# One sum of a vector over the partitions by two rounded matmuls instead of an exact one, in a two-layer hybrid decoder on one Trainium2 core

## The reference

```python
c_act = jax.nn.silu(c)
for i in range(DEPTH):                       # 2 layers
    mod = c_act @ ada_w[i] + ada_b[i]        # 1024 -> 9 * 1024
    sh1, sc1, gt1, sh2, sc2, gt2, sh3, sc3, gt3 = jnp.split(mod, N_MOD, axis=-1)
    h = h + 0.5 * gt1 * swiglu(modulate(h, sh1, sc1), ffn_w_gu[i, 0], ffn_w_down[i, 0])
    h = h + gt2 * mixer(modulate(h, sh2, sc2))
    h = h + 0.5 * gt3 * swiglu(modulate(h, sh3, sc3), ffn_w_gu[i, 1], ffn_w_down[i, 1])
# swiglu: gate, up = split(x @ w_gu); (silu(gate) * up) @ w_down, with D_FF = 2816
```

## Time and profile before

| | us |
|---|---|
| median of three runs (1491.93, 1502.3, 1502.09) | 1502.09 |
| the profiled execution | 1490.03 |
| its span | 1488.3 |
| PE busy | 1277.8 (86%) |
| DVE busy | 959.1 (64%) |
| ACT busy | 542.0 (36%) |

### The profile page before, as it was taken

The page is one execution under the profiler, slowest core; times in us unless marked ns, Lnnn a source line. Parts: engine busy times, 40 slices in busy tenths (PEclk is TensorE's granted clock), DMA queues, the critical chain, the costliest instruction groups (busy, mean ns, idle before and its releaser), DMA issues.

```text
span 1488.3 us, 17063 instructions
## 1 busy us (share of the span) xinstructions
PE 1277.8 (86%) x6370; PEld 1017.5 (68%) x6370; DVE 959.1 (64%) x1242; ACT 542.0 (36%) x733; POOL 77.9 (5%) x68
## 2 busy tenths in 40 slices
PE   5899998785988999989999868775836995899998
PEld 1588887662566888867888744664835994688886
DVE  5787776876448877768787563367592338554553
ACT  2434345342344344354343434352501002344431
POOL 1000000000000000000000000005350005000000
PEclk9899999895589999999999987887756555999999
DMA  8798874830018988757888541310102011465551
GB/s 310 250 316 299 295 253 149 282 114 1 0 57 283 313 299 291 263 189 267 291 303 296 143 121 57 113 57 1 29 0 57 2 58 58 140 226 170 169 198 57
DMA packets 186753, 252.17 MB, mean 169 GB/s; under 512 B 31489, under 2 KB 122625, under 8 KB 186689
## 3 DMA queue, kind: packets, MB, share of 16 engines
q1 hardware_dynamic: 186690, 251.32, 50.3%
HBM read 249.19 MB, written 2.10 MB: 169 GB/s over the span
## 4 chain that ended last, share of the span: by engine, by line
PE 72%; DVE 17%; DMA 4%; ACT 4%; issue 2%; SPq 2%; POOL 0%; DVEq 0%; ACTq 0%; POOLq 0%
PE bank L709 18%; PE bank L711 18%; PE bank L710 18%; DVE inv_tmp L1795 2%; DVE gu_lo L1610 2%; DVE ada_acc L1543 2%; PE bank L910 2%; PE bank L1120 2%; PE bank L682 1%; PE bank L1128 1%; PE bank L768 1%; ACT gu_hi L1178 1%; PE bank L920 1%; PE bank L937 1%; DVE inv_out L1797 1%
## 5 line engine op out<-in xcount | busy, mean ns | idle before, releaser
L709 PE MATMUL bank<-gu_hi,xT_hi 128*128 128x512 f32 (+1 forms) x880 | 352.4, 400 | 32.1 <-DVE gu_lo L1610 10.8
L710 PE MATMUL bank<-gu_lo,xT_hi 128*128 128x512 f32 (+1 forms) x880 | 350.1, 398 | 0.0
L711 PE MATMUL bank<-gu_hi,xT_lo 128*128 128x512 f32 (+1 forms) x880 | 349.5, 397 | 0.0
L1610 DVE TENSOR_TENSOR gu_lo<-raw,gu_hi 128x2048 fp32r<-128x2048 f32 (+1 forms) x116 | 257.6, 2255 | 60.7 <-ACT gu_hi L1178 60.7
L1178 ACT CAST gu_hi<-raw 128x2048 fp32r<-128x2048 f32 (+1 forms) x116 | 215.4, 1884 | 36.1 <-DMA raw<-in_ffn_w_gu_dram 23.5
L709 PEld LDWEIGHTS bank<-gu_hi,xT_hi 128*128 128x128 f32 x880 | 170.8, 194 | 74.5 <-issue 14.6
L710 PEld LDWEIGHTS bank<-gu_lo,xT_hi 128*128 128x128 f32 x880 | 170.7, 194 | 37.4 <-issue 0.7
L711 PEld LDWEIGHTS bank<-gu_hi,xT_lo 128*128 128x128 f32 x880 | 170.5, 194 | 35.9
L1543 DVE SCALAR_TENSOR_TENSOR ada_acc<-ada_raw,cact,ada_acc 128x512 f32<-128x512 f32 x224 | 168.4, 752 | 12.3 <-DMA ada_raw<-in_ada_w_dram 1.0
L709 PE MATMUL bank<-dn_hi,hT_hi 128*128 128x512 f32 x320 | 142.9, 447 | 2.6 <-DVE dn_lo L1620 2.6
L1196 ACT ACTIVATE hid<-bank 128x256 f32<-128x256 f32 x88 | 33.3, 380 | 291.3 <-PE bank L711 291.3
(11 more groups left out here) (267 smaller groups left out, 1619.2 us busy)
## 6 DMA issues: line engine op xcount, KB each, us to landing
raw<-in_ffn_w_gu_dram SPq DMA_DIRECT2D x176, 512.0 KB, 9.0
ada_raw<-in_ada_w_dram SPq DMA_DIRECT2D x128, 512.0 KB, 6.9
raw<-in_ffn_w_down_dram SPq DMA_DIRECT2D x40, 1024.0 KB, 5.0
raw<-in_rwkv_w_rkv_dram SPq DMA_DIRECT2D x24, 512.0 KB, 5.2
raw<-in_dsa_w_in_dram SPq DMA_DIRECT2D x16, 512.0 KB, 5.0
front<-in_ada_w_dram SPq DMA_DIRECT2D x8, 512.0 KB, 8.0
front<-in_ada_w_dram SPq DMA_DIRECT2D x4, 1024.0 KB, 13.8
last_raw<-in_ffn_w_down_dram SPq DMA_DIRECT2D x4, 1024.0 KB, 6.4
```

Source lines behind the costliest of these rows:

```text
L709: nc.tensor.matmul(out_ap, sta_hi, mov_hi, start=start, stop=False, skip_group_check=True)
L710: nc.tensor.matmul(out_ap, sta_hi, mov_lo, start=False, stop=False, skip_group_check=True)
L711: return nc.tensor.matmul(out_ap, sta_lo, mov_hi, start=False, stop=stop, skip_group_check=True)
L1610: nc.vector.tensor_tensor(gu_lo[:, par, ks, 0:width], buf[:, i, 0:4 * width].rearrange("p (k c) -> p k c", k=4), gu_hi[:, par, ks, 0:width ...
```

## The change

Three things change.

1. In the FFNs (not in the attention) the sum over the partitions is made by two matmuls in the rounded format. ACT casts `ada_acc` to `acc_hi` (`round_acc`), DVE subtracts to get `acc_lo` (`rest_of_acc`), and PE multiplies a rounded matrix of ones by both (`ffn_total`). `acc_hi` and `acc_lo` lie in the place of `xn`. `round_acc` stands on ACT ahead of `round_down`, `rest_of_acc` on DVE ahead of `rest_of_down`.
2. Before the first FFN, vector 3 has four products on PE and four on DVE instead of two and six; vector 2 is loaded in one transfer instead of two; the second half of weight block 0 is split (ACT and DVE) ahead of `first_x(2)` and `first_x(3)` instead of behind them; on PE the sum of vector 3 and two transposes move by a few matmuls.
3. At the entry of the third FFN, `ffn(2)`, ACT casts the second weight block around `deviation(q, 1)` instead of behind `turned_tile(q, 1)`.

```diff
-    FRONT_PIECES = (4, 2, 2, 4)
-    ON_PE = 2
+    FRONT_PIECES = (4, 2, 1, 4)
+    ON_PE = (2, 2, 2, 4)
+            def ffn_total(f, b):
+                u = ADA_DONE[f] + b
+                pe.wait_ge(acc_ready, u + 1)
+                nc.tensor.matmul(TB[0][:], ones_r[:], acc_hi[:], start=True, stop=False)
+                nc.tensor.matmul(TB[0][:], ones_r[:], acc_lo[:], start=False, stop=True).then_inc(ada_sum, 1)
@@ first_gate_up (PE)
-                gate_up(0, 0, 0, ks=range(0, 2))
+                gate_up(0, 0, 0, ks=range(0, 4))
                 front_total(3)
-                gate_up(0, 0, 0, ks=range(2, 4))
                 pe.wait_ge(xT_ready, 2)
-                gate_up(0, 0, 1, ks=range(0, 2))
-                turn_x(0, range(2, 3))
-                gate_up(0, 0, 1, ks=range(2, 4))
-                turn_x(0, range(3, 4))
+                gate_up(0, 0, 1, ks=range(0, 4))
+                turn_x(0, range(2, 4))
@@ ffn, step (PE)
                             pe.wait_ge(hT_ready[0], ub)
-                            ada_total(v0 + b - 1, TB[0])
+                            ffn_total(f, b - 1)
                         down(f, ub - 1, 0, peeled and b == 1)
@@ ACT
+            def round_acc(v):
+                act.wait_ge(ada_step, (v - ADA_FRONT) * KD + KD)
+                nc.scalar.copy(acc_hi[:], ada_acc[:]).then_inc(acc_hi_ready, 1)
@@ ffn (ACT)
+                if f == 2:
+                    act.wait_ge(g_ready[1], n0)
+                    round_block(n0 + 1, (n0 + 1) % 2, free=True, halves=range(0, 1))
                 if f:
                     deviation(q, 1)
+                if f == 2:
+                    round_block(n0 + 1, (n0 + 1) % 2, free=True, halves=range(1, 2))
+                if f:
                     turned_tile(q, 1)
@@ step (ACT)
                         silu(n - 1, ub - 1, 1, peeled and ub == 1)
                         round_hidden(ub - 1, 0, peeled and ub == 1)
+                        if nv and not (peeled and b > nv):
+                            round_acc(v0 + b - 1)
                         round_down(f, ub - 1, peeled and ub == 1)
-                    round_block(n + 1, (n0 + odd + 1) % 2, peeled and n == 0)
+                    if not (peeled and b == 0 and f == 2):
+                        round_block(n + 1, (n0 + odd + 1) % 2, peeled and n == 0)
@@ start (ACT)
             round_block(0, 0, True, halves=range(0, 1))
+            round_block(0, 0, True, halves=range(1, 2))
             copy_mods(3, FRONT[3][0], TB[1])
-            round_block(0, 0, True, halves=range(1, 2))
@@ first_modulate (DVE)
                 front_products(3)
+                rest_of_block(0, 0, halves=range(1, 2))
                 dve.wait_ge(mods_ready, 4)
                 first_x(2)
                 first_x(3)
-                rest_of_block(0, 0, halves=range(1, 2))
@@ step (DVE)
+            def rest_of_acc(f, b):
+                dve.wait_ge(acc_hi_ready, ADA_DONE[f] + b + 1)
+                nc.vector.tensor_tensor(acc_lo[:], ada_acc[:], acc_hi[:].bitcast(F32), ALU.subtract).then_inc(acc_ready, 1)
                         rest_of_hidden(ub - 1, 0)
+                        if nv and not (peeled and b > nv):
+                            rest_of_acc(f, b - 1)
                         rest_of_down(f, ub - 1)
```

More of the change, by code:

```diff
@@ L64, in trunk @@
     FRONT = ((2, 0), (0, 2), (3, 1), (1, 3))
-    FRONT_PIECES = (4, 2, 2, 4)
-    ON_PE = 2
+    FRONT_PIECES = (4, 2, 1, 4)
+    ON_PE = (2, 2, 2, 4)
     ADA_FFN = ((4, 10), (17, 10), (27, 9), (36, 0))
+    ADA_DONE = tuple(sum(n for _, n in ADA_FFN[:f]) for f in range(4))
     ADA_DSA = 14
@@ L116, in trunk @@
         chunk_decay = place("chunk_decay", [P, KD, NC])
+        ones_r = place("ones_r", [P, P], F32R, at=top["at"])
         rstat = place("rstat", [P, 128])
@@ L127, in trunk @@
         xn_at = top["at"]
+        acc_hi = place("acc_hi", [P, HALF], F32R, at=xn_at)
+        acc_lo = place("acc_lo", [P, HALF], F32R, at=xn_at + 2048)
         xn = place("xn", [P, 2, HALF])
@@ L140, in trunk @@
         front_acc = [ada_acc[:], hid[:].rearrange("p t c -> p (t c)")]
-        c_wide = place("c_wide", [P, 2, P], at=spare_at)
+        c_wide = place("c_wide", [P, ON_PE[-1], P], at=spare_at)
         last_raw = place("last_raw", [P, 2, D], at=ada_at)
@@ L231, in trunk @@
         ada_sum = sem("ada_sum")
+        acc_hi_ready = sem("acc_hi_ready")
+        acc_ready = sem("acc_ready")
         mods_ready = sem("mods_ready")
@@ L688, in front_products @@
                     pe.wait_ge(mods_ready, j - 1)
-                pe.wait_ge(front_in[j][0], 16)
-                for k in range(ON_PE):
+                for k in range(ON_PE[j]):
+                    if k % 2 == 0:
+                        pe.wait_ge(front_in[j][k * len(front_in[j]) // KD], 16)
                     nc.tensor.matmul(spread[:], c_wide[:, k, :], front[:, FRONT[j][1], k, :], start=k == 0, stop=False)
             def front_total(j):
-                pe.wait_ge(front_step, (j + 1) * (KD - ON_PE))
+                pe.wait_ge(front_step, sum(KD - n for n in ON_PE[:j + 1]))
                 nc.tensor.matmul(TB[j % 2][:], ones[:], front_acc[j % 2], start=False, stop=True).then_inc(ada_sum, 1)
+            def ffn_total(f, b):
[3 more added lines that the diff above has]
+                nc.tensor.matmul(TB[0][:], ones_r[:], acc_lo[:], start=False, stop=True).then_inc(ada_sum, 1)
             def turn_x(q, parts=range(4)):
@@ L837, in ffn @@
                     pe.wait_ge(hT_ready[0], last)
-                    ada_total(v0 + nv - 1, TB[0])
+                    ffn_total(f, nv - 1)
                 down(f, last - 1, 0, False)
@@ L1153, in _ @@
             pe.wait_ge(consts, 6)
-            pe.wait_ge(c_ready, 2)
+            pe.wait_ge(c_ready, 3)
             for j in range(3):
@@ L1475, in ffn @@
                 round_hidden(last - 1, 0)
+                if nv == NB - 1:
+                    round_acc(v0 + nv - 1)
                 round_down(f, last - 1, False)
@@ L1498, in _ @@
             nc.scalar.activation(cact[:], ccol[:], ACT.Silu).then_inc(c_ready, 1)
-            nc.scalar.activation(c_wide[:], ccol[:, 0:ON_PE].unsqueeze(2).broadcast_to([P, ON_PE, P]), ACT.Silu
+            nc.scalar.activation(c_wide[:], ccol[:, 0:ON_PE[-1]].unsqueeze(2).broadcast_to([P, ON_PE[-1], P]), ACT.Silu
                                  ).then_inc(c_ready, 1)
             act.wait_ge(consts, 6)
+            nc.scalar.copy(ones_r[:], ones[:]).then_inc(c_ready, 1)
             copy_mods(0, FRONT[0][0], TB[0])
@@ L1552, in front_products @@
                 total = front_acc[j % 2]
-                for k in range(ON_PE, KD):
+                for k in range(ON_PE[j], KD):
                     if k % 2 == 0:
                         dve.wait_ge(front_in[j][k * FRONT_PIECES[j] // KD], 16)
-                    if k > ON_PE:
-                        dve.wait_ge(front_step, j * (KD - ON_PE) + k - ON_PE)
+                    if k > ON_PE[j]:
+                        dve.wait_ge(front_step, sum(KD - n for n in ON_PE[:j]) + k - ON_PE[j])
                     nc.vector.scalar_tensor_tensor(out=total, in0=front[:, slot, k, :], scalar=cact[:, k:k + 1],
-                                                   in1=total if k > ON_PE else front_bias[:, hv, :],
+                                                   in1=total if k > ON_PE[j] else front_bias[:, hv, :],
                                                    op0=ALU.mult, op1=ALU.add).then_inc(front_step, 1)
@@ L1901, in ffn @@
                 rest_of_hidden(last - 1, 0)
+                if nv == NB - 1:
+                    rest_of_acc(f, nv - 1)
                 rest_of_down(f, last - 1)
```

## The result

| | median | runs | ratio to the kernel before | profiled execution |
|---|---|---|---|---|
| kernel before | 1490.35 us | 13, 1486.44 to 1502.3 | | 1490.03 us, span 1488.3 |
| changed kernel | 1507.51 us | 13, 1502.05 to 1518.35 | 1.011 [1.0081, 1.0139] | 1507.55 us, span 1505.8 |

The account below looks back on a forecast made before the run. PE was taken to bound an FFN block at 17.80 us, after the change a ring of 18.0 us; +0.5 + 5.7 + 3.1 = +9.3 us on the median of the runs shown gave 1511.4 us, range 1497 to 1514.

Parts of the forecast that it names:

- the ring: First three FFNs: last product, rounding, `dn_hi`, `dn_lo`, down load issue, landing, products wait in a circle, 18.0 us a block.
- the 4.99 us from last product to issue: One leg of the ring: rounding 0.53 us, semaphore 0.06, cast to down load issue 4.40; about 5.0 us.
- TensorE's wait for `dn_lo`: In each block ahead of `down`, PE was to wait some 0.6 us for `dn_lo`.
- The PE-bound rival: The ring closes below 17.40 us, PE stays the bound: -14.8 us, 1487.3 us; chance 0.10.
- The transpose at "about 54 us": First FFN's entry: the transpose at 58.29 us was to come at about 54 us, through the earlier weight split.
- the first down load at 65.7: First FFN: block 1's down load issued at 65.7 instead of 67.93 us, -2.2 us.
- The third FFN's early casts: Third FFN's entry: casts moved into ACT's idle time let DVE start `gu_lo` 1.0 us earlier.
- the leg from issue to last product: Other leg of the ring, down load issue to the modulation's last product: taken as 13.0 us, mean 13.40.
- the first FFN was forecast at +0.5 us: First FFN's last product at 222.7 us instead of 222.2, after eight ring periods and one more leg.
- the second at +5.7: Second FFN's last product at 633.05 instead of 627.31 us, all of it going through to the tail.
- the third at +3.1: Third FFN's last down load of the ring issued at 826.6 instead of 823.45 us.
- The rival with a stretched ring: Issue to last product stays at 13.4 us, the ring is 18.4 us: +19.7 us, 1521.8 us; chance 0.25.

Follow-up runs that it names:

- E5: Kernel before with exact sums, only ACT made to wait for the vector's last product ahead of the down weights' cast: 1500.67 us, ratio 1.0053.
- E7: Changed kernel with the modulation loads issued on SP ahead of the wait for the down buffer, from block 1 on: 1483.17 us, ratio 0.9947.
- the opened kernels: E4, E7 and E8, changed kernels with the ring cut at one link or two; a steady block is 17.36 us in all three.
- E6: Changed kernel with the rounding done twice, one after the other, same values: 1522.91 us, ratio 1.0199.
- E2: Kernel before with only the new order before the first FFN (part 2 of the change): 1488.11 us, ratio 0.9979.
- E10: Changed kernel, ring still closed, with the first sum of each FFN left exact: 1502.03 us, ratio 1.0059.
- E9: E8 with the first sum of each FFN left exact: 1473.38 us, ratio 0.9866 to the kernel before.
- E8: Changed kernel with both openings, those of E4 and E7: 1482.43 us, ratio 0.9946.
- E4: Changed kernel with the rounding behind the down weights' cast on ACT and its rest behind `dn_lo` on DVE: 1485.5 us, ratio 0.9967.

## Why the prediction was right in kind and too small

**Right: the ring.** Its links, their order and the 4.99 us from last product to issue all stand in the trace (4.96; the rounding and its semaphore, for which no row was shown, take 134.17 - 133.61 = 0.56 us of them, 0.59 forecast). TensorE's wait for `dn_lo` is 18.2 us in all, 0.7 us a block (0.6 forecast), and E5 and E7 show the ring from both sides: the wait without the work costs, the work without the circle does not. The PE-bound rival is out for the change as it is, and exact for the opened kernels (17.40 said, 17.36 measured).

**Right: the moved steps.** The transpose at "about 54 us" is at 54.33, the first down load at 65.7 is at 65.87. In the second FFN the down load follows the last product by 4.8 us, 5.0 forecast. The third FFN's early casts gave 1.5 us until its products, 1.0 forecast.

**Mis-sized: the leg from issue to last product.** It was put at 13.0 us, against its own mean of 13.40, with the reason that "a ring that is longer than 17.8 us leaves the queue more time to empty". Measured it is 13.26 on the mean, and 14.3 us in the last leg of the first FFN. By stages: the first FFN was forecast at +0.5 us and came to +1.7, all of the excess in that last leg; the second at +5.7 and came to +7.7, with eight periods 2.2 longer than forecast; the third at +3.1 and came to +5.6 (its periods 3.0 longer than forecast, its entry 0.6 shorter). That is 5.7 of the 8.2 us that the traces have beyond the forecast. The means of E5, of the change and of E6 show that the reason itself was wrong. The rival with a stretched ring had 18.4 us and +19.7; the second and third FFN lie nearer to it than to the forecast, and its chance of 0.25 was too low. As a ratio, +1.1% stands just on its side of the 1% line.

**Missing: a term for the clock.** Between the first FFN's last product and the second FFN's first ones the changed kernel lost 2.5 us more, and the prediction held the tail to pass the shift on as it is. Windows there, first the kernel before, then the changed one:

```profile
233.00:239.00 6.00, 6.00 (x28) 4.93 (x27) 2.61 (x5) 2.08 (x4) 0.00 (x0) 1.00 0.99 344
...
254.70:265.00 10.30, 8.90 (x35) 8.00 (x34) 8.79 (x9) 4.79 (x7) 0.00 (x0) 0.50 0.63 223
```

```profile
235.00:238.40 3.40, 3.40 (x10) 2.65 (x9) 0.48 (x2) 1.16 (x2) 0.00 (x0) 0.50 0.99 369
...
255.50:269.20 13.70, 11.25 (x42) 9.98 (x43) 10.91 (x12) 5.98 (x8) 0.00 (x0) 0.50 0.69 247
```

The same tail has 10.3 us at the lower level (1.2 GHz) before and 17.1 us after. In 235.00 to 238.40 PE is fully busy, behind waits of 1.5 and 2.1 us for `dn_lo` and in its own sequencer. No run was made to part the two waits, the moved end of the FFN and the clock, but the traces on record say which it goes with. E6 has the ring, a `dn_lo` wait of 2.04 us and one of 1.45 us in the sequencer in the same place, and full clock from the first of them on until the 10.2 us at the lower level that the kernel before has as well:

```profile
238.40:265.00 26.60, 22.48 (x115) 18.17 (x116) 17.55 (x30) 13.27 (x27) 0.00 (x0) 1.00 0.43 136
```

It needs 248.5 us from the first FFN's last product to the second's first ones, where the kernel before needs 248.9 and the changed one 251.4. E2, which rounds nothing, has 250.4 us, and there the stretch at the lower level is over 13 us long instead of 10.3 (its window 249.50 to 262.50 has 0.50). So the 2.5 us go with the clock, and neither the rounding nor a wait of 2 us brings it about by itself.

That the first blocks of the FFNs ran slow as well (windows of 6 us from the first `down` on have 0.57, 0.72 and 0.56) cost the changed kernel little: the ring closed later anyway. E10 has 1.00 there and gained little more than its entry term (5.2 us against 4.6, by the traces). In the opened kernels the same stretch was on the path, and E9 against E8 is its price.

**Open.** What makes the modulation's landing take 6.4 us in one block and 7.7 in another: the bytes and the order of the queue are the same in both. And E4 against E7, 2.3 us, less than their intervals tell apart.

## What to carry to other kernels

When a wait is put ahead of an instruction on an in-order engine, follow what stands behind it through every in-order queue until it either ends or comes back to the wait; if it comes back, the period is the sum of the links, no engine's share shows it, and moving one instruction behind its neighbour (22 us here, E4 against the change) can be worth more than making it faster. Price a link that varies by its mean in the trace, not by its best cases and a reason why they should become the rule. And before an instruction is made cheaper everywhere, look at the first round apart: there the cheap form's latency can be on the path though its steady form is hidden.

## What the runs showed of the hardware

**A wait of under 3 us can be followed by twice its length at half the clock.** In the first block of an FFN, behind waits of PE for 2.70 us (the changed kernel) or 2.79 us (E8), the windows of 6 us show a granted clock of 0.50 to 0.72 in each of the three FFNs; behind 1.16 us (E9, E10) they show 1.00. But the length of the wait does not decide it alone: in the third FFN of the kernel before, waits of 0.80 and 1.16 us are followed by 0.74, and E6 in the tail has 1.00 behind 2.04 us.

```profile
681.67:687.67 6.00, 6.00 (x20) 4.79 (x21) 4.92 (x4) 0.00 (x0) 0.00 (x0) 0.74 0.85 297
```

In the first two FFNs of E8 the loss of wait and clock together was more than twice the 1.6 us by which the wait was too long.

**Part of the scatter between runs of one kernel goes with the clock.** In the RWKV mixer, whose instructions are the same in all these kernels, the clock differs from one profiled execution to another. One stretch of it, from the issue of the load `ln<-in_rwkv_ln_b_dram` to that of the first `out_raw<-in_rwkv_w_out_dram`, is shown here, first of the kernel before (profiled 1490.03 us, median 1490.35), then of E8 (profiled 1493.79, median 1482.43):

```profile
1128.22:1210.86 82.64, 79.21 (x961) 76.53 (x962) 20.60 (x30) 9.27 (x16) 0.00 (x0) 0.58 0.06 15
```

```profile
1122.27:1214.59 92.32, 89.40 (x961) 86.22 (x962) 20.65 (x30) 9.26 (x16) 0.00 (x0) 0.50 0.05 14
```

The same 961 matmuls take 9.7 us more where the whole stretch is at the lower level. The kernel before has 13.6 us at the full clock in it:

```profile
1138.80:1152.40 13.60, 12.04 (x218) 11.36 (x218) 3.38 (x5) 3.71 (x7) 0.00 (x0) 1.00 0.00 1
```

The profiled executions of E2 (1498.1 us, median 1488.11) and E4 (1494.88, median 1485.5) are like E8's, with 92.3 us each; those of the changed kernel and of E9 are like the other, with 82.7 and 82.6. That this clock explains all of the scatter was not shown. A profiled execution can therefore stand on either side of its kernel's median, and stages have to be compared by their own length, not by the total.
